# Six places instead of four for split weights, up to the third gate-up block

## The chip, the cores and the metric

One core of a Trainium2 chip runs the kernel. The metric is the device time of one execution in microseconds (us); lower is better. Engines: PE is TensorE (PEld its weight loads), DVE is VectorE, ACT is ScalarE, POOL is GpSimd, SP is SyncE, whose queue issues most of the DMAs.

## The reference

One layer of a decoder trunk with 256 positions and a width of 1024, in float32: three attention branches, a gated merge, and a SwiGLU feed-forward part.

```python
h = rms_norm(x, pre_mix_g[l])
mem_n = rms_norm(mem, mem_norm_g[l])
y = hybrid_mixer(h, mem_n, ...)      # h @ w_in (1024 x 5400), three branches, merge, w_mix_out
x = x + rms_norm(y, post_mix_g[l])
h = rms_norm(x, pre_ffn_g[l])
f = (jax.nn.silu(h @ w_ffn_gate[l]) * (h @ w_ffn_up[l])) @ w_ffn_down[l]   # inner width 2816
x = x + rms_norm(f, post_ffn_g[l])
```

In the mixer the compressed branch of NSA takes its keys and values (the columns `k_c`, `v_c` of `h @ w_in`), joins windows of 32 positions and multiplies them by `cmp_w1` and `cmp_w2`. The selected and window branches, MoBA and the memory branch attend over 256 keys each.

## The kernel before

Every large product has to be more exact than one pass in the fast format (fp32r). So each weight w is split in two fp32r numbers, `wh` (w rounded, written by ACT in `hi`) and `wl` = w - `wh` (written by DVE in `lo`), and the activations likewise (`xh`, `xl`). PE then does three matmuls for one product (`product`, L1120 to L1122): xh by wh, xh by wl, xl by wh.

The weights stream through in units of 1 MB, in one fixed order, on SP's queue, into `raw`, which has `RAW` = 4 slots. A unit is two parts of 256 rows by 512 columns; part v is half of unit v // 2. Part v goes this way: SP loads its unit; ACT makes `wh` in one of `SUBS` = 4 places (`hi`, L474) once the unit has landed (`loaded`) and PE is done with the part that had the place before (`mm_done`); DVE makes `wl` (`lo`, L761); PE multiplies (`sub`, 12 matmuls of 512 columns). A raw slot is free once DVE has split both its parts (`free_slot` on SP).

A block is 512 columns of output. In the first stage each has four parts: block 0 parts 0 to 3, block 1 parts 4 to 7, block 2 parts 8 to 11, and so on. The sums of a block lie in one of two places in PSUM (`acc`), one bank for each tile of 128 positions. ACT copies the bank of tile 0 to `pat` and DVE the bank of tile 1 (`evac_cols`, L556 and L856), and each then raises `ev[0]` or `ev[1]`. PE starts block b only when block b - 2 is copied (`free_acc`).

Each engine runs its own list, written out by hand, in that order alone. `hi_to(v)` and `lo_to(v)` put into ACT's and DVE's list all splits up to part v that are not yet there. In `evac_cols(b)` the first statement is `hi_to(v_last + AHEAD)` (on DVE `lo_to(v_last + AHEAD)`), with v_last the block's last part and `AHEAD` = `SUBS` - 1; the copy stands behind these splits:

```python
v_last = 4 * b + 3
hi_to(v_last + AHEAD)
act.wait_ge(rstd_done, 2 if b >= B_MEMKV else 1)
wait_block(b, 0, v_last)
```

After the first part of block 2 (part 8), PE turns the columns of block 1 that hold `k_c` and `v_c` (`qk_batch(0, 2, ...)`, four 128x128 transposes, L1231). It waits for `ev[0]` and `ev[1]` of block 1 first:

```python
for t in range(TILES):
    pe.wait_ge(ev[t], blocks_ready)
```

The order of loads on SP's queue in this stage is: units 0 and 1 with parts of `gx`, units 2 and 3, `x` (1 MB), units 4 and 5, `memt` (1 MB), units 6 and 7, `mem` (1 MB), units 8 and 9, and `tb` (1.5 MB). Unit 4 waits for the split of unit 0, unit 5 for that of unit 1, and so on. POOL's queue loads `cmp_w1` (2 MB) once block 0 is done. So part 10 is in unit 5, and part 12 in unit 6.

Later stages: 24 attention jobs (`job_plan`) with a gate part between each pair of steps, the merge of branches, the mix block, 11 gate-up blocks in a hardware loop (`ffn_act`, `ffn_dve`, `ffn_body`), and the down projection. At a job n the lists have `hi_to(V_GATE + n + AHEAD)` and `lo_to(V_GATE + n + look_ahead(n))`. `V_GATE` = 24, `V_GU` = 64.

Of the kernel before, what the change touches and what calls it, by code (L numbers as in the profile page):

```python
# [56 lines left out]
ATT_TAIL = ATT_W - 4 * SLICE  # L57
RAW, SUBS = 4, 4
AHEAD = SUBS - 1

# [56 lines left out]
def build_layer(nc, a, out, g_scratch):  # L117
# [13 lines left out]
    with ExitStack() as ctx:  # L131
# [328 lines left out]
        def _(act):  # L460
# [6 lines left out]

            def hi(v, slot, half, w, first_load):

                act.wait_ge(loaded[slot], first_load)  # L470
                if not (isinstance(v, int) and v < SUBS):
                    act.wait_ge(mm_done, v - SUBS + 1)
                k = (2 * slot + half) % SUBS
                nc.scalar.activation(wh[:, k, :, 0:w], raw[:, slot, 2 * half:2 * half + 2, 0:w], ACT.Copy).then_inc(hi_done, 1)  # L474

            def first_hi(k):

                if k < 2:
# [5 lines left out]
                nc.scalar.activation(wh[:, k // 2, k % 2], raw[:, k // 4, k % 4], ACT.Copy).then_inc(hi_done, 1)  # L484
# [43 lines left out]
            for k in range(PIECES):  # L528
                x_hi(k)
                first_hi(k)  # L530
            split[0] = SUBS

# [160 lines left out]
            roots(2, 1, 2)  # L693
            hi_to(V_GU + 3)
            for j in (2, 3):
# [11 lines left out]
            def ffn_hi(i, j, s):  # L707

                v = V_GU + AHEAD + s + 4 * i
                vj = AHEAD + s + 4 * j  # L710
                hi(v, (vj // 2) % RAW, vj % 2, SLICE, ((V_GU + vj) // 2 // RAW + 1) * 32 + (i - j) * 16)

# [4 lines left out]

            def ffn_act(i, j, first):
                for s in range(4):
                    if not first:  # L720
                        ffn_hi(i, j, s)
                    if s == 2 and not first:
                        ffn_ah(i - 1)
# [15 lines left out]
            split[0] = V_GU + 4 * GU_BLOCKS + AHEAD  # L739
            hi_to(V_DOWN + 2 + AHEAD)  # L740
            ffn_ah(GU_BLOCKS - 1)
            nc.scalar.preload_act_table(ACT.Sqrt)
            for n in range(2):
                v_last = V_DOWN + 11 * n + 10
                hi_to(v_last + AHEAD)
# [8 lines left out]
        def _(dve):  # L754
            split = [0]

            def lo(v, slot, half, w):

                dve.wait_ge(hi_done, v + 1 + SUBS)
                k = (2 * slot + half) % SUBS  # L760
                nc.vector.tensor_tensor(wl[:, k, :, 0:w], raw[:, slot, 2 * half:2 * half + 2, 0:w],  # L761
                                        wh[:, k, :, 0:w].bitcast(F32), ALU.subtract).then_inc(lo_done, 1)

            def first_lo(k):

                dve.wait_ge(hi_done, k + 1)
                nc.vector.tensor_tensor(wl[:, k // 2, k % 2], raw[:, k // 4, k % 4], wh[:, k // 2, k % 2].bitcast(F32),
                                        ALU.subtract).then_inc(lo_done, 1)

            def lo_to(v_end):  # L770
                while split[0] <= min(v_end, 2 * UNITS - 1):
                    v = split[0]
                    lo(v, v // 2 % RAW, v % 2, width(v))
                    split[0] += 1
# [47 lines left out]
            for k in range(PIECES):  # L822
                x_lo(k)
                first_lo(k)
            split[0] = SUBS
            dve.wait_ge(bias_row, 1)
# [221 lines left out]
            for t in range(TILES):  # L1048
                gain(0, 0, t, B_MIX)
            lo_to(V_MIX + 7)  # L1050
# [5 lines left out]
            lo_to(V_GU + 1)  # L1056
            round_lo(3, 0)
            lo_to(V_GU + 2)
            sum_halves(0, 1)
# [3 lines left out]
            add_residual(0, 1, 0, 2, x1_done)  # L1063
            lo_to(V_GU + 3)
            add_residual(0, 1, 1, 2, x1_done)
# [15 lines left out]

            def ffn_dve(i, j, first):
                for s in range(4):
                    if not first:
                        ffn_lo(i, j, s)
                    if s == 2 and not first:
                        ffn_al(i - 1)
# [6 lines left out]

            ffn_dve(0, 0, True)
            with nc.vector.Fori(0, (GU_BLOCKS - 1) // 2) as it:
                for j in range(2):
                    ffn_dve(it * 2 + (1 + j), 1 - j, False)
            split[0] = V_GU + 4 * GU_BLOCKS + AHEAD
            lo_to(V_DOWN + 2 + AHEAD)  # L1100
            ffn_al(GU_BLOCKS - 1)
            dve.wait_ge(gpostd, 32)
            lo_to(V_DOWN + 10 + AHEAD)
            for t in range(TILES):
# [11 lines left out]
        def _(pe):  # L1116
# [7 lines left out]
            def sub(v, slot, parity, h, l, k0, w, first, last):  # L1124

                pe.wait_ge(lo_done, v + 1 + SUBS)
                for t in range(TILES):
# [14 lines left out]
            def whole_block(b, v0, subs, h, l, k0=0, w=SLICE, ready=None, after=None):  # L1142
# [3 lines left out]
                for i in range(subs):  # L1146
                    if ready is not None:
                        ready(i)
                    sub(v0 + i, (v0 + i) % SUBS, b % 2, h, l, k0 + 2 * i, w, i == 0, i == subs - 1)
                    for work in (after or {}).get(i, ()):  # L1150
                        work()

            def first_block(after):

                for k in range(PIECES):
                    slot, s = k // 2, k % 2
                    pe.wait_ge(hi_done, k + 1)
# [15 lines left out]
            def by_tiles(b, v0, subs, h, l, k0, ready=None, after=None, first=True):  # L1173
# [3 lines left out]
                for t in range(TILES):  # L1177
                    for i in range(subs):
                        v = v0 + i
                        if t == 0:  # L1180
                            pe.wait_ge(lo_done, v + 1 + SUBS)
                        if ready is not None and i % 2 == 0:
                            pe.wait_ge(tl_done, ready + 2 * t + i // 2 + 1)
                        for s in range(2):
                            ins = product(acc[:, b % 2, t], h, l, k0 + 2 * i + s, t, v % SUBS, s, SLICE,
                                          first and i == 0 and s == 0, i == subs - 1 and s == 1)
# [177 lines left out]
            for n in range(JOBS + 2):  # L1364
# [41 lines left out]
            for n in range(2):  # L1406
                v, b = V_NSA + 2 * n, B_NSA + n
                free_acc(b)
                sub(v, v % SUBS, b % 2, oh, ol, 4, SLICE, True, False)
# [4 lines left out]
                sub(v + 1, (v + 1) % SUBS, b % 2, oh, ol, 6, SLICE, False, True)  # L1414
            whole_block(B_MIX, V_MIX, 4, xh, xl, ready=lambda i: pe.wait_ge(tl_done, i + 1),
# [6 lines left out]
            def ffn_body(i, j, first):  # L1422
# [82 lines left out]
```

## Time and profile before

| what | value |
|---|---|
| time, median of 3 runs | 420.07 us (419.51 to 420.63) |
| the profiled execution's own time | 419.44 us |
| its span, first to last instruction | 417.6 us |
| PE busy | 408.4 us, 98% of the span |
| PEld, DVE, ACT, POOL busy | 328.3, 260.5, 233.5, 40.2 us |
| DMA moved | 78.82 MB, mean 189 GB/s |

The 1.8 us between the span and the profiled time lie ahead of the first and behind the last instruction. A matmul's modelled end overlaps the start of the next, so the step from start to start tells PE's rate: 0.23 us for 512 columns in fp32r.

### The profile page before, as it was taken

What the parts mean: (1) busy time and instruction counts of PE and PEld (TensorE: products, weight loads), DVE (VectorE), ACT (ScalarE), POOL (GpSimd) and SP (SyncE); (2) the same over time, 40 slices, a digit from 0 to 9 for tenths busy, and PEclk for the clock granted to TensorE, in tenths of its full rate; (3) what the DMA queues carried; (4) which work ended last, traced back from release to release, by engine and by line L of the source; (5) the groups of instructions that cost most, each with busy time, mean ns of one, the idle gap of its engine ahead of it and who ended that gap; (6) DMA issues with size and microseconds to landing.
All of it is one profiled execution on the core that took longest, in us unless ns stands there. A gap on an engine that the chain in (4) does not pass through costs nothing.

```text
span 417.6 us, 5875 instructions
## 1 busy us (share of the span) xinstructions
PE 408.4 (98%) x2070; PEld 328.3 (79%) x2070; DVE 260.5 (62%) x450; ACT 233.5 (56%) x402; POOL 40.2 (10%) x76
## 2 busy tenths in 40 slices
PE   8999999999999999999999999999999999999994
PEld 4787889877777777877787788888888888888883
DVE  4854965875776786649859665556555655545434
ACT  5654964577767766744646774544554454545321
POOL 3210020021212122126000000000000000000000
PEclk9999999999999999999999999999999999999999
DMA  8999993535344335366555467556655556666002
GB/s 294 393 335 369 375 334 111 194 112 191 112 152 141 100 104 199 102 239 215 193 173 165 138 227 227 169 176 196 201 178 169 174 185 198 202 202 193 9 0 100
DMA packets 52016, 78.82 MB, mean 189 GB/s; under 512 B 2076, under 2 KB 28488, under 8 KB 51992
## 3 DMA queue, kind: packets, MB, share of 16 engines
q1 hardware_dynamic: 50216, 73.52, 53.7%
q0 software_dynamic: 1344, 4.43, 3.2%
q10 hardware_dynamic: 432, 0.56, 0.4%
q8 instruction: 14, 0.23, 0.2%
q14 instruction: 10, 0.08, 0.1%
HBM read 77.43 MB, written 1.07 MB: 188 GB/s over the span
## 4 chain that ended last, share of the span: by engine, by line
PE 92%; DVE 2%; ACT 2%; DMA 1%; issue 1%; ACTq 0%; DVEq 0%
PE acc L1120 27%; PE acc L1122 26%; PE acc L1121 26%; PE ob L1361 3%; PE sbank L1310 3%; PE ptb L1324 2%; DMA gx<-in_gx 1%; PE ptb L1439 1%; PE acc L1159 1%; PE sbank L1231 1%; PE acc L1163 1%; DVE gates L951 1%; PE acc L1164 1%; DVE xl L796 1%; ACT xh L507 0%
## 5 line engine op out<-in xcount | busy, mean ns | idle before, releaser
L761 DVE TENSOR_TENSOR wl<-raw,wh 128x1024 fp32r<-128x1024 f32 (+1 forms) x126 | 152.7, 1218 | 92.9 <-ACT wh L474 92.4
L474 ACT ACTIVATE wh<-raw 128x1024 fp32r<-128x1024 f32 (+1 forms) x126 | 131.0, 1046 | 92.6 <-PE acc L1122 80.5
L1120 PE MATMUL acc<-wh,xh 128*128 128x512 f32 (+1 forms) x368 | 146.3, 398 | 1.1 <-DVE xl L796 1.1
L1122 PE MATMUL acc<-wh,xl 128*128 128x512 f32 (+1 forms) x368 | 142.2, 386 | 0.0
L1121 PE MATMUL acc<-wl,xh 128*128 128x512 f32 (+1 forms) x368 | 142.0, 386 | 0.0
L1120 PEld LDWEIGHTS acc<-wh,xh 128*128 128x128 f32 x368 | 69.1, 188 | 18.0 <-issue 4.9
L1122 PEld LDWEIGHTS acc<-wh,xl 128*128 128x128 f32 x368 | 69.1, 188 | 14.3
L1121 PEld LDWEIGHTS acc<-wl,xh 128*128 128x128 f32 x368 | 69.2, 188 | 12.5
L1120 PE MATMUL acc<-wh,ah 128*128 128x512 f32 x88 | 34.3, 390 | 0.0
L1122 PE MATMUL acc<-wh,al 128*128 128x512 f32 x88 | 34.3, 389 | 0.0
L1121 PE MATMUL acc<-wl,ah 128*128 128x512 f32 x88 | 34.2, 389 | 0.0
L440 POOL TENSOR_SCALAR sx<-sx,jst 128x256 f32<-128x256 f32 (+1 forms) x48 | 20.2, 433 | 94.2 <-DVE jst L987 52.4
L649 ACT ACTIVATE sx<-sx,jst 128x128 f32<-128x128 f32 (+1 forms) x40 | 17.9, 451 | 5.3 <-DVE jst L979 5.3
L1122 PEld LDWEIGHTS acc<-wh,al 128*128 128x128 f32 x88 | 16.5, 188 | 3.5
L1121 PEld LDWEIGHTS acc<-wl,ah 128*128 128x128 f32 x88 | 16.5, 188 | 3.4
L1120 PEld LDWEIGHTS acc<-wh,ah 128*128 128x128 f32 x88 | 16.5, 188 | 3.3
L731 ACT ACTIVATE silu<-acc,rstd 128x256 f32<-128x256 f32 x22 | 10.3, 475 | 11.8 <-DVE act_tok L1092 8.0
L969 DVE TENSOR_TENSOR sx<-sbank,tb 128x128 f32<-128x128 f32 (+1 forms) x40 | 12.4, 352 | 6.5 <-PE sbank L1310 4.9
L627 ACT ACTIVATE pts<-ptb 128x512 f32<-128x512 f32 x16 | 9.6, 599 | 10.0 <-PE ptb L1324 9.9
L1092 DVE SCALAR_TENSOR_TENSOR act_tok<-acc,rstd,silu 128x256 f32<-128x256 f32 x22 | 10.5, 481 | 6.8 <-ACT silu L731 6.8
L1120 PE MATMUL acc<-wh,oh 128*128 128x512 f32 x32 | 12.9, 402 | 0.0
L677 ACT ACTIVATE tmp<-acc 128x512 f32<-128x512 f32 x8 | 4.8, 600 | 14.2 <-PE acc L1122 14.2
(187 smaller groups left out, 407.0 us busy)
## 6 DMA issues: line engine op xcount, KB each, us to landing
raw<-in_w_in SPq DMA_DIRECT2D x18, 1024.0 KB
raw<-in_w_ffn_gate SPq DMA_DIRECT2D x22, 512.0 KB
raw<-in_w_ffn_up SPq DMA_DIRECT2D x22, 512.0 KB
raw<-in_w_ffn_down SPq DMA_DIRECT2D x22, 512.0 KB
raw<-in_w_mix_out SPq DMA_DIRECT2D x4, 1024.0 KB
raw<-in_w_mem_kv SPq DMA_DIRECT2D x2, 1024.0 KB
raw<-in_w_nsa_o SPq DMA_DIRECT2D x2, 1024.0 KB
raw<-in_w_in SPq DMA_DIRECT2D x3, 512.0 KB, 7.2
```

The source lines that it names most:

```text
L440: ins = nc.gpsimd.tensor_scalar(sx[:, n % 2, lo:hi], sx[:, n % 2, lo:hi], jst[:, 4, n, t:t + 1], 1.0, ALU.mult, ALU.mult)
L474: nc.scalar.activation(wh[:, k, :, 0:w], raw[:, slot, 2 * half:2 * half + 2, 0:w], ACT.Copy).then_inc(hi_done, 1)
L649: ins = nc.scalar.activation(sx[:, n % 2, lo:hic], src[:, n % 2, lo:hic], ACT.Exp, bias=jst[:, 1, n, t:t + 1], scale=SCALE, accum_out=jst[ ...
L731: nc.scalar.activation(silu[:, t], acc[:, j % 2, t, 0:GU_W], ACT.Silu, scale=rstd[:, 3, t:t + 1]).then_inc(silu_done, 1)
L761: nc.vector.tensor_tensor(wl[:, k, :, 0:w], raw[:, slot, 2 * half:2 * half + 2, 0:w], wh[:, k, :, 0:w].bitcast(F32), ALU.subtract).then_in ...
L969: nc.vector.tensor_tensor(sx[:, n % 2, c0:c1], sbank[:, n % 2, c0:c1], tb[:, bh, c1 - c0 - 1::-1], ALU.add).then_inc(dve_c, 1)
L1092: nc.vector.scalar_tensor_tensor(act_tok[:, t], acc[:, j % 2, t, GU_W:2 * GU_W], rstd[:, 3, t:t + 1], silu[:, t], ALU.mult, ALU.mult).then ...
L1120: nc.tensor.matmul(bank[:, 0:w], h[:, k, c], wh[:, slot, s, 0:w], start=first, stop=False)
L1121: nc.tensor.matmul(bank[:, 0:w], h[:, k, c], wl[:, slot, s, 0:w], start=False, stop=False)
L1122: return nc.tensor.matmul(bank[:, 0:w], l[:, k, c], wh[:, slot, s, 0:w], start=False, stop=last)
L1310: ins = nc.tensor.matmul(sbank[:, side, c0:c1], qt[half_rows(side), q, P * t:P * t + P], kt[half_rows(side), k, 0:c1 - c0], start=True, st ...
L1361: ins = nc.tensor.matmul(ob[half_rows(side), c0:c1], v, p, start=(i == 0), stop=(i == count - 1))
```

## The change

The ring of places for split weights has six places (`SUBS` = 6) for all parts up to the end of the third gate-up block, and goes back to four (`FFN_SUBS` = 4) behind it. `AHEAD` goes from 3 to 5, so that ACT and DVE split two parts further ahead in all calls that name `AHEAD`. Calls with a plain number (`hi_to(11)`, `lo_to(15)` and others in the first stage) stay as they are; those at the mix block are written out two parts later. `hi` is given its place and the place's last user. Where `SUBS` stood for the four parts that are split in eight pieces at the start, `IN_PIECES` = 4 stands now. The second and third gate-up blocks are taken out of ACT's and DVE's loops, with 4 and 2 splits (`FFN_PARTS`). `tmp`, which takes what the squares write and nobody reads, shares its place in SBUF with `silu` and `act_tok`. `raw` still has 4 slots, and SP's and POOL's lists are as before.

```diff
-RAW, SUBS = 4, 4
-AHEAD = SUBS - 1
+RAW, SUBS, FFN_SUBS, IN_PIECES = 4, 6, 4, 4
+AHEAD, FFN_AHEAD = SUBS - 1, FFN_SUBS - 1
+FFN_PARTS = [[V_GU + 9, V_GU + 10, V_GU + 11, V_GU + 12], [V_GU + 13, V_GU + 14]]
+def ring(v):
+    w = v - V_GU
+    return w % SUBS if w < 2 * SUBS else w % FFN_SUBS
+def last_user(v):
+    return v - SUBS if v - V_GU < 2 * SUBS + FFN_SUBS else v - FFN_SUBS
-            tmp = sb("tmp", [P, TILES, SLICE], F32, late)
+            with ExitStack() as early:
+                tmp = sb("tmp", [P, TILES, SLICE], F32, early)
-            def hi(v, slot, half, w, first_load):
+            def hi(v, k, slot, half, w, first_load, user):
                 act.wait_ge(loaded[slot], first_load)
-                if not (isinstance(v, int) and v < SUBS):
-                    act.wait_ge(mm_done, v - SUBS + 1)
-                k = (2 * slot + half) % SUBS
+                if not (isinstance(user, int) and user < 0):
+                    act.wait_ge(mm_done, user + 1)
...
-                    hi(v, u % RAW, v % 2, width(v), 32 * (u // RAW + 1))
+                    hi(v, ring(v), u % RAW, v % 2, width(v), 32 * (u // RAW + 1), last_user(v))
...
-            hi_to(V_MIX + 7)
+            hi_to(V_GU + 1)
             squares(0, 1, 0, B_MIX + 1, V_MIX + 7)
...
-            hi_to(V_GU + 1)
+            hi_to(V_GU + 3)
             round_hi(3, 0)
-            hi_to(V_GU + 2)
+            hi_to(V_GU + 4)
...
-            ffn_act(0, 0, True)
-            with nc.scalar.Fori(0, (GU_BLOCKS - 1) // 2) as it:
+            ffn_act(0, 0, True, ())
+            ffn_act(1, 1, False, FFN_PARTS[0])
+            ffn_act(2, 0, False, FFN_PARTS[1])
+            with nc.scalar.Fori(0, (GU_BLOCKS - 3) // 2) as it:
                 for j in range(2):
-                    ffn_act(it * 2 + (1 + j), 1 - j, False)
+                    ffn_act(it * 2 + (3 + j), 1 - j, False)
```

ACT's list around the copies of blocks 0 and 1, before. The first `pat` row is the copy of block 0, the second that of block 1, which stands behind the splits of parts 7 to 10; `gcmp` is what is made of the transposed `k_c` columns:

```order
L525 ACTIVATE small<-ssq,eps 128x2 [waits ssq_done]
L556 ACTIVATE pat<-acc,rstd 128x2x4x64 [waits acc0_done,rstd_done]
L474 ACTIVATE wh<-raw 128x1024 [waits mm_done,loaded3]
L474 ACTIVATE wh<-raw 128x1024 [waits mm_done,loaded0] x2
L474 ACTIVATE wh<-raw 128x1024 [waits mm_done,loaded1]
L556 ACTIVATE pat<-acc,rstd 128x512 [waits acc0_done,rstd_done]
L474 ACTIVATE wh<-raw 128x1024 [waits mm_done,loaded1]
L569 ACTIVATE gcmp<-sbank 64x16x15 [waits qk_pe]
L569 ACTIVATE gcmp<-sbank 64x16x15 x3
L474 ACTIVATE wh<-raw 128x1024 [waits mm_done,loaded2]
L561 ACTIVATE qt<-sbank 128x512 [waits qk_pe]
```

So four splits stand between the two copies, and none between `small` and the copy of block 0. The same stretch of ACT's list in the changed kernel:

```order
L538 ACTIVATE small<-ssq,eps 128x2 [waits ssq_done]
L487 ACTIVATE wh<-raw 128x1024 [waits mm_done,loaded3]
L487 ACTIVATE wh<-raw 128x1024 [waits mm_done,loaded0]
L569 ACTIVATE pat<-acc,rstd 128x2x4x64 [waits acc0_done,rstd_done]
L487 ACTIVATE wh<-raw 128x1024 [waits mm_done,loaded0]
L487 ACTIVATE wh<-raw 128x1024 [waits mm_done,loaded1] x2
L487 ACTIVATE wh<-raw 128x1024 [waits mm_done,loaded2]
L569 ACTIVATE pat<-acc,rstd 128x512 [waits acc0_done,rstd_done]
L582 ACTIVATE gcmp<-sbank 64x16x15 [waits qk_pe]
L582 ACTIVATE gcmp<-sbank 64x16x15 x3
L574 ACTIVATE qt<-sbank 128x512 [waits qk_pe]
```

The splits of parts 11 and 12 moved ahead of the copy of block 1; the one of part 12 waits for `loaded2`, which is unit 6.

DVE's list at the end of the first stage, before, from the copies that end the compressed keys (`ckeys`, `pat<-ob`) to the first step of the compressed softmax (`xc`):

```order
L916 COPY ckeys<-ob 64x15 x2
L919 COPY pat<-ob 32x2x64 x4
L761 TENSOR_TENSOR wl<-raw,wh 128x1024 x2
L856 TENSOR_SCALAR pat<-acc,rstd 128x280
L930 TENSOR_TENSOR xc<-ob,tbc 128x2x4x15
```

The same place in the changed kernel:

```order
L932 COPY ckeys<-ob 64x15 x2
L935 COPY pat<-ob 32x2x64 x4
L777 TENSOR_TENSOR wl<-raw,wh 128x1024 x4
L872 TENSOR_SCALAR pat<-acc,rstd 128x280
L946 TENSOR_TENSOR xc<-ob,tbc 128x2x4x15
```

Four splits instead of two now stand between the copies and the 280 columns of block 5.

## Rows read from the trace of the kernel before

**Rows 1.** The page: busy us of each engine, share of the span, instructions.
```profile
PE 408.4 (98%) x2070; PEld 328.3 (79%) x2070; DVE 260.5 (62%) x450; ACT 233.5 (56%) x402; POOL 40.2 (10%) x76
```

**Rows 2.** Waits of PE, whole span: us in total, times, longest.
```profile
PE acc L1120 <- DVE xl L796: 1.1, 2, 0.7
PE ptb L1280 <- DVE eps L817: 0.9, 1, 0.9
PE sbank L1205 <- DVE yb L955: 0.7, 1, 0.7
PE sbank L1231 <- issue: 0.6, 1, 0.6
PE ptb L1205 <- DVE yb L955: 0.2, 1, 0.2
```

**Rows 3.** Timeline of PE: start, duration, instruction, and idle time before it.
```profile
31.68 0.39 PE L1122 MATMUL acc<-wh,xl 128*128 128x512 f32 x1
32.64 0.41 PE L1231 MATMUL sbank<-const,pat 128*128 128x128 f32 x2 [0.58 <-issue]
```

**Rows 4.** Timeline of ACT, 29 to 41 us.
```profile
29.56 1.06 ACT L474 ACTIVATE wh<-raw 128x1024 fp32r<-128x1024 f32 x1 [4.37 <-DMA raw<-in_w_in]
30.53 0.67 ACT L556 ACTIVATE pat<-acc,rstd 128x512 f32<-128x512 f32 x1
...
33.31 1.55 ACT L569 ACTIVATE gcmp<-sbank 64x240 f32<-64x240 f32 x4 [1.16 <-PE ptb L1231]
39.81 1.06 ACT L474 ACTIVATE wh<-raw 128x1024 fp32r<-128x1024 f32 x1 [4.94 <-DMA raw<-in_w_in]
```

**Rows 5.** Timeline of DVE, 30 to 41 us.
```profile
30.66 1.22 DVE L761 TENSOR_TENSOR wl<-raw,wh 128x1024 fp32r<-128x1024 f32 x1 [3.82 <-ACT wh L474]
31.80 0.74 DVE L856 TENSOR_SCALAR pat<-acc,rstd 128x512 f32<-128x512 f32 x1
...
40.90 1.22 DVE L761 TENSOR_TENSOR wl<-raw,wh 128x1024 fp32r<-128x1024 f32 x1 [5.65 <-ACT wh L474]
```

**Rows 6.** Two stretches: length, busy PE, PEld, DVE, ACT, POOL (count), PEclk, DMA share, GB/s.
```profile
30.00:42.00 12.00, 11.42 (x57) 9.20 (x56) 5.65 (x8) 5.83 (x10) 0.53 (x1) 1.00 1.05 362
240.00:410.00 170.00, 170.00 (x772) 140.67 (x772) 91.02 (x99) 82.43 (x103) 0.00 (x0) 1.00 0.53 167
```

**Rows 7.** DMA issues: queue, count, KB, us to landing; then SP's queue, timeline.
```profile
memt<-in_memt SPq DMA_DIRECT2D x1, 1024.0 KB, 20.6
...
16.49 0.39 SPq L355 DMA_DIRECT2D memt<-in_memt  x1
18.38 11.36 SPq L322 DMA_DIRECT2D raw<-in_w_in  x2
```

**Rows 8.** PE at the start; one chain piece; PE's last matmul; two stretches as rows 6.
```profile
0.94 4.63 PE L1280 MATMUL ptb<-eps 128*128 128x512 f32 x6 [0.94 <-DVE eps L817]
6.34 0.40 PE L1163 MATMUL acc<-wl,xh 128*128 128x512 f32 x1
...
36.04 0.44 PE sbank L1231 x4
...
411.74 0.39 PE L1122 MATMUL acc<-wh,al 128*128 128x512 f32 x1
...
412.20:415.80 3.60, 0.00 (x0) 0.00 (x0) 2.24 (x5) 0.95 (x3) 0.00 (x0) 1.00 0.26 98
415.80:417.60 1.80, 0.00 (x0) 0.00 (x0) 0.00 (x0) 0.00 (x0) 0.00 (x0) 0.51 0.53 199
```

**Rows 9.** Timelines of DVE and PE where the first attention job starts.
```profile
76.45 0.51 DVE L856 TENSOR_SCALAR pat<-acc,rstd 128x280 f32<-128x280 f32 x1
81.24 0.17 DVE L990 RECIPROCAL jst<-jst 128x2 f32<-128x2 f32 x1 [1.05 <-ACT sx L649]
...
80.97 0.60 PE L1231 MATMUL ob<-const,pat 128*128 128x128 f32 x4
84.16 0.49 PE L1324 MATMUL ptb<-const,sx 128*128 128x128 f32 x3
```

More of the change, by code:

```diff
@@ L483, in first_hi @@
                     act.wait_ge(loaded[k // 4], 32)
-                nc.scalar.activation(wh[:, k // 2, k % 2], raw[:, k // 4, k % 4], ACT.Copy).then_inc(hi_done, 1)
+                nc.scalar.activation(wh[:, ring(k // 2), k % 2], raw[:, k // 4, k % 4], ACT.Copy).then_inc(hi_done, 1)
             def hi_to(v_end):
@@ L530, in _ @@
                 first_hi(k)
-            split[0] = SUBS
+            split[0] = IN_PIECES
             def squares_of(i, src, t):
@@ L693, in _ @@
             roots(2, 1, 2)
-            hi_to(V_GU + 3)
+            hi_to(V_GU + 5)
             for j in (2, 3):
@@ L707, in ffn_hi @@
             def ffn_hi(i, j, s):
-                v = V_GU + AHEAD + s + 4 * i
-                vj = AHEAD + s + 4 * j
-                hi(v, (vj // 2) % RAW, vj % 2, SLICE, ((V_GU + vj) // 2 // RAW + 1) * 32 + (i - j) * 16)
+                v = V_GU + FFN_AHEAD + s + 4 * i
+                vj = FFN_AHEAD + s + 4 * j
+                hi(v, vj % FFN_SUBS, (vj // 2) % RAW, vj % 2, SLICE, ((V_GU + vj) // 2 // RAW + 1) * 32 + (i - j) * 16, v - FFN_SUBS)
             def ffn_ah(i):
@@ L716, in ffn_ah, with ffn_act @@
                 nc.scalar.activation(ah[:, bass.ds(i * 2, 2), :], ptb[:], ACT.Copy).then_inc(ah_done, 1)
-            def ffn_act(i, j, first):
+            def ffn_act(i, j, first, parts=None):
                 for s in range(4):
-                    if not first:
+                    if parts is None:
                         ffn_hi(i, j, s)
+                    elif s < len(parts):
+                        hi_to(parts[s])
                     if s == 2 and not first:
@@ L734, in _ @@
             act.wait_ge(rstd_done, 5)
-            ffn_act(0, 0, True)
-            with nc.scalar.Fori(0, (GU_BLOCKS - 1) // 2) as it:
+            ffn_act(0, 0, True, ())
+            ffn_act(1, 1, False, FFN_PARTS[0])
+            ffn_act(2, 0, False, FFN_PARTS[1])
+            with nc.scalar.Fori(0, (GU_BLOCKS - 3) // 2) as it:
                 for j in range(2):
-                    ffn_act(it * 2 + (1 + j), 1 - j, False)
-            split[0] = V_GU + 4 * GU_BLOCKS + AHEAD
-            hi_to(V_DOWN + 2 + AHEAD)
+                    ffn_act(it * 2 + (3 + j), 1 - j, False)
+            split[0] = V_GU + 4 * GU_BLOCKS + FFN_AHEAD
+            hi_to(V_DOWN + 2 + FFN_AHEAD)
             ffn_ah(GU_BLOCKS - 1)
@@ L744, in _ @@
                 v_last = V_DOWN + 11 * n + 10
-                hi_to(v_last + AHEAD)
+                hi_to(v_last + FFN_AHEAD)
                 for t in range(TILES):
@@ L755, in _, with lo @@
             split = [0]
-            def lo(v, slot, half, w):
-                dve.wait_ge(hi_done, v + 1 + SUBS)
-                k = (2 * slot + half) % SUBS
+            def lo(v, k, slot, half, w):
+                dve.wait_ge(hi_done, v + 1 + IN_PIECES)
                 nc.vector.tensor_tensor(wl[:, k, :, 0:w], raw[:, slot, 2 * half:2 * half + 2, 0:w],
@@ L766, in first_lo @@
                 dve.wait_ge(hi_done, k + 1)
-                nc.vector.tensor_tensor(wl[:, k // 2, k % 2], raw[:, k // 4, k % 4], wh[:, k // 2, k % 2].bitcast(F32),
+                nc.vector.tensor_tensor(wl[:, ring(k // 2), k % 2], raw[:, k // 4, k % 4], wh[:, ring(k // 2), k % 2].bitcast(F32),
                                         ALU.subtract).then_inc(lo_done, 1)
@@ L772, in lo_to @@
                     v = split[0]
-                    lo(v, v // 2 % RAW, v % 2, width(v))
+                    lo(v, ring(v), v // 2 % RAW, v % 2, width(v))
                     split[0] += 1
@@ L824, in _ @@
                 first_lo(k)
-            split[0] = SUBS
+            split[0] = IN_PIECES
             dve.wait_ge(bias_row, 1)
@@ L1049, in _ @@
                 gain(0, 0, t, B_MIX)
-            lo_to(V_MIX + 7)
+            lo_to(V_GU + 1)
             sum_halves(0, 0)
@@ L1055, in _ @@
                 add_residual(0, 0, n, 2, x1_done)
-            lo_to(V_GU + 1)
+            lo_to(V_GU + 3)
             round_lo(3, 0)
-            lo_to(V_GU + 2)
+            lo_to(V_GU + 4)
             sum_halves(0, 1)
@@ L1063, in _ @@
             add_residual(0, 1, 0, 2, x1_done)
-            lo_to(V_GU + 3)
+            lo_to(V_GU + 5)
             add_residual(0, 1, 1, 2, x1_done)
@@ L1073, in ffn_lo @@
             def ffn_lo(i, j, s):
-                vj = AHEAD + s + 4 * j
-                lo(V_GU + AHEAD + s + 4 * i, (vj // 2) % RAW, vj % 2, SLICE)
+                vj = FFN_AHEAD + s + 4 * j
+                lo(V_GU + FFN_AHEAD + s + 4 * i, vj % FFN_SUBS, (vj // 2) % RAW, vj % 2, SLICE)
             def ffn_al(i):
@@ L1080, in ffn_al, with ffn_dve @@
                                         ah[:, bass.ds(i * 2, 2), :].bitcast(F32), ALU.subtract).then_inc(al_done, 1)
-            def ffn_dve(i, j, first):
+            def ffn_dve(i, j, first, parts=None):
                 for s in range(4):
-                    if not first:
+                    if parts is None:
                         ffn_lo(i, j, s)
+                    elif s < len(parts):
+                        lo_to(parts[s])
                     if s == 2 and not first:
@@ L1093, in ffn_dve @@
                                                    silu[:, t], ALU.mult, ALU.mult).then_inc(prod_done, 1)
-            ffn_dve(0, 0, True)
-            with nc.vector.Fori(0, (GU_BLOCKS - 1) // 2) as it:
+            ffn_dve(0, 0, True, ())
+            ffn_dve(1, 1, False, FFN_PARTS[0])
+            ffn_dve(2, 0, False, FFN_PARTS[1])
+            with nc.vector.Fori(0, (GU_BLOCKS - 3) // 2) as it:
                 for j in range(2):
-                    ffn_dve(it * 2 + (1 + j), 1 - j, False)
-            split[0] = V_GU + 4 * GU_BLOCKS + AHEAD
-            lo_to(V_DOWN + 2 + AHEAD)
+                    ffn_dve(it * 2 + (3 + j), 1 - j, False)
+            split[0] = V_GU + 4 * GU_BLOCKS + FFN_AHEAD
+            lo_to(V_DOWN + 2 + FFN_AHEAD)
             ffn_al(GU_BLOCKS - 1)
             dve.wait_ge(gpostd, 32)
-            lo_to(V_DOWN + 10 + AHEAD)
+            lo_to(V_DOWN + 10 + FFN_AHEAD)
             for t in range(TILES):
@@ L1124, in sub @@
             def sub(v, slot, parity, h, l, k0, w, first, last):
-                pe.wait_ge(lo_done, v + 1 + SUBS)
+                pe.wait_ge(lo_done, v + 1 + IN_PIECES)
                 for t in range(TILES):
@@ L1148, in whole_block @@
                         ready(i)
-                    sub(v0 + i, (v0 + i) % SUBS, b % 2, h, l, k0 + 2 * i, w, i == 0, i == subs - 1)
+                    sub(v0 + i, ring(v0 + i), b % 2, h, l, k0 + 2 * i, w, i == 0, i == subs - 1)
                     for work in (after or {}).get(i, ()):
@@ L1155, in first_block @@
                 for k in range(PIECES):
-                    slot, s = k // 2, k % 2
+                    slot, s = ring(k // 2), k % 2
                     pe.wait_ge(hi_done, k + 1)
@@ L1180, in by_tiles @@
                         if t == 0:
-                            pe.wait_ge(lo_done, v + 1 + SUBS)
+                            pe.wait_ge(lo_done, v + 1 + IN_PIECES)
                         if ready is not None and i % 2 == 0:
@@ L1184, in by_tiles @@
                         for s in range(2):
-                            ins = product(acc[:, b % 2, t], h, l, k0 + 2 * i + s, t, v % SUBS, s, SLICE,
+                            ins = product(acc[:, b % 2, t], h, l, k0 + 2 * i + s, t, ring(v), s, SLICE,
                                           first and i == 0 and s == 0, i == subs - 1 and s == 1)
@@ L1382, in _ @@
                         free_acc(b)
-                    sub(V_GATE + n, n % SUBS, b % 2, xh, xl, 2 * i, SLICE, i == 0, i == 3)
+                    sub(V_GATE + n, ring(V_GATE + n), b % 2, xh, xl, 2 * i, SLICE, i == 0, i == 3)
                 if n == 0:
@@ L1408, in _ @@
                 free_acc(b)
-                sub(v, v % SUBS, b % 2, oh, ol, 4, SLICE, True, False)
+                sub(v, ring(v), b % 2, oh, ol, 4, SLICE, True, False)
                 if n == 0:
@@ L1413, in _ @@
                     merged_banks(0, 2)
-                sub(v + 1, (v + 1) % SUBS, b % 2, oh, ol, 6, SLICE, False, True)
+                sub(v + 1, ring(v + 1), b % 2, oh, ol, 6, SLICE, False, True)
             whole_block(B_MIX, V_MIX, 4, xh, xl, ready=lambda i: pe.wait_ge(tl_done, i + 1),
@@ L1427, in ffn_body @@
                 for s in range(4):
-                    sub(i * 4 + (V_GU + s), s, j, xh, xl, 2 * s, SLICE, s == 0, s == 3)
+                    slot = ring(4 * i + V_GU + s) if isinstance(i, int) else s
+                    sub(i * 4 + (V_GU + s), slot, j, xh, xl, 2 * s, SLICE, s == 0, s == 3)
                     if s == 1:
@@ L1452, in _ @@
                     v = V_DOWN + 11 * n + i
-                    sub(v, v % SUBS, (B_DOWN + n) % 2, ah, al, 2 * i, SLICE, i == 0, i == 10)
+                    sub(v, ring(v), (B_DOWN + n) % 2, ah, al, 2 * i, SLICE, i == 0, i == 10)
                     if n == 0 and i == 1:
```

## The prediction

> **What bounds the kernel now.** I read the engines' busy times first, then PE's waits, then the timelines of PE, ACT and DVE where PE waits. PE is busy for 408.4 of 417.6 us [rows 1]; the other engines have a third or more of their time free, so what PE does sets the end, and any time in which PE stands adds to it one for one. PE's list of waits is short: five rows, 3.5 us in all [rows 2]. One of them, 0.9 us, is the wait for the very first operand. The other four, 2.6 us, are the most that work done further ahead could give back, and none of the five names a split weight (`wl` or `wh`) as what came last. In the feed-forward stretch from 240 to 410 us PE is busy for 170.00 of 170.00 us [rows 6]. So PE never stands for want of the split weights in what these views show, and a deeper ring for them has nothing there to win.
>
> The row that matters is PE's stop before L1231. Its last matmul of part 8 starts at 31.68 us, the transposes of `k_c` and `v_c` start at 32.64 us, and 0.58 us of it is idle [rows 3]. The profile calls it "issue", but the code says what PE waits for: the copies of block 1 on ACT and on DVE. ACT waits 4.37 us for unit 5 to land, splits part 10 from 29.56 us, and copies from 30.53 us [rows 4]; DVE splits part 10 from 30.66 us and copies from 31.80 to 32.54 us [rows 5]. PE goes on 0.10 us later. The reader sees here a copy that is late only because it stands in an in-order list behind a split whose data have not landed. From the start of ACT's last split ahead of the copy to PE's restart it is 32.64 - 29.56 = 3.08 us.
>
> **The change, part by part.** *ACT and DVE around block 1.* The change puts the splits of parts 11 and 12 ahead of the copy of block 1, as the order of ACT's list shows. Part 11 is in unit 5, as part 10 is, and costs one split. Part 12 is in unit 6. ACT splits it before at 39.81 us, after 4.94 us of idle time that ends with the landing [rows 4], so 39.81 us is when unit 6 landed. Does the change bring unit 6 earlier? The list on SP's queue is the same. The unit needs slot 2, free after the split of part 5, which stands where it stood; SP issued it at 18.38 us, behind `memt`, issued at 16.49 us with 20.6 us to land, so at 37.1 us [rows 7]. The DMA engines are full over this stretch, with a busy share of 1.05 from 30 to 42 us [rows 6]. Unit 6 comes 2.7 us behind `memt` on a queue that is full, and nothing that the change moves is ahead of it. I take 39.81 us, and 0.7 us to either side.
>
> The tail of the chain is the same as before: the last split on ACT, then the last split on DVE, then DVE's copy, then PE. So PE restarts at 39.81 + 3.08 = 42.89 us instead of 32.64 us. **Term 1: +10.25 us.** Since L1231 stands in PE's list ahead of parts 9 to 11, all of PE's work is behind it, and nothing of PE's can be done meanwhile. The 0.58 us of before is inside the 10.25, not beside it.
>
> *PE's clock after the stop.* PE would stand from about 32.07 (31.68 + 0.39) to 42.89 us, 10.8 us. No such stop is in the trace before, but its end and its start bound the cost. After the last matmul, which ends at about 412.13 us, the granted clock stays at 1.00 up to 415.80 us and is then 0.51 [rows 8], 3.7 us behind PE's last work. A stop of 10.8 us is nearly three times that, so I expect the lower level, 1.2 GHz, at the restart. How long does it last? At the start, six matmuls of 512 columns on `eps` begin in 0.94 us and take 4.63 us, 0.77 us or more each; four transposes of the same plain float32 kind with 128 columns take 0.44 us in the chain at 36.04 us, 0.11 us each, which is 0.44 us for 512 columns [rows 8]. The first six thus run at half speed, and full speed is there at 6.34 us at the latest, after at most 5.4 us of work. Work done at half speed for 5.4 us costs 2.7 us more than at full speed; for the 4.63 us, 2.3 us. The bounds are 0 (the level does not fall) and 2.7 us; since rows 8 show both the fall and the slow start, I take the upper half, 2.4 us. **Term 2: +2.4 us.**
>
> By the Trainium skill (TensorE: Matmul & The Clock Gate, HAM oscillation), a long wait for DMA between matmuls drops the array to half clock, and the matmuls after it run cold. The trace shows the drop only at its end, where nothing follows; no row before shows a cold restart in mid-kernel. Without that rule and without rows 8 the sum would be 2.4 us less.
>
> *Blocks 0 and 2 to 4.* Block 0 now waits for part 8, in unit 4. PE needs that copy only at block 2, some 5 us later: 0. The copy of block 2 waits for part 16 in unit 8; DMA goes on during PE's stop and so is 10 us further against PE: 0. In ACT's and DVE's lists between there are calls with plain numbers, which keep their reach, so the copy of block 3 comes in a bunch of four splits. Each is about 1.2 us on DVE [rows 5]; two more than before, 2.4 us, of which the delay of PE's restart hides most. I take 0, with 1 us as the upper bound.
>
> *Block 5 and the first job.* DVE now has two more splits ahead of the copy of block 5, 2 x 1.2 = 2.4 us. That copy starts at 76.45 us, the reciprocal of job 0 comes at 81.24 us, and PE turns job 0 at 84.16 us; the transposes of `q_x` at 80.97 us want the copy of block 5 and the end of `xc` [rows 9]. In DVE's own list the reciprocal moves by some 1.8 to 2.4 us, to 83.4 at the latest, and GpSimd's scaling and a hand-over after it take about 1 us: 84.4 against 84.16. So this is nearly all in the slack. **Term 3: +0.1 us**, bounds 0 and 1.5.
>
> *The rest.* From job 1 on each call does as many splits as before, since the lead was gained once; each still waits for the same `mm_done`, because the reach and the number of places grow by the same 2. The waits for `yb` and `xl` (0.7, 0.2 and 1.1 us) [rows 2] come from copies and sums that the change does not touch: 0, and at most 2.0 us to gain. `raw` has four slots and each slot is freed two parts earlier and needed two parts earlier: 0. `tmp` has no reader, so a shared place costs 0. The unrolled gate-up blocks have 6 splits instead of 8 in a stretch where PE never stands: 0; if that cover were gone, a split on ACT is 1.06 us [rows 4].
>
> **Sum.** 10.25 + 2.4 + 0.1 = 12.75 us on the profiled execution's 419.44 us: 432.2 us. The median of the runs is 0.63 us above that execution (420.07 against 419.44), so the median after is 432.8 us, 3.0% slower.
>
> **The rivals.**
> A. *As above*, a stop of about 10 us and a slow restart: 432.8 us. Chance 0.70.
> B. *The stop without the slow restart*: the clock's fall needs more than 10.8 us, or full speed is back at once. 420.07 + 10.35 = 430.4 us. For it: nothing shows a fall in mid-kernel. Against it: the 3.7 us at the end. Chance 0.10.
> C. *The late bunches cost too*: the copy of block 3 or of block 5 is late for PE, by up to 1 and 1.5 us: up to 435.3 us. For it: DVE's slack at job 0 is used up. Against it: PE is later by all of the first stop. Chance 0.10.
> D. *Unit 6 lands sooner*, since a place for a split and so a slot comes free earlier somewhere, and the stop is 3 to 8 us: 423 to 430 us. Against it: part 5, and all that is ahead of unit 6, stand where they stood. Chance 0.05.
> E. *Faster*: the deeper lead gives back waits for split weights that hide in the modelled ends, and the copy of block 1 is not late. Its place is L1231; it needs unit 6 before about 29 us, so that 3.08 us later PE is not held at 32.1 us. Then the most is the 2.6 us of rows 2: 417.5 us. Chance 0.03. *No change* is the same with nothing to give back: 420.1 us, 0.02.
>
> A difference under 0.3% (1.3 us) is about what a measurement of this kernel cannot tell from none. Slower has 0.95 (A to D), the same 0.02, faster 0.03. The likeliest case by itself spans 431.2 to 434.0 (unit 6 by 0.7 us, the clock by 1.1 and 0.3). The range takes in B and most of C: 429.8 to 435.0 us.
>
> **What the profile after would show.** Term 1: ACT's copy of block 1 behind a split that ends an idle stretch "<-DMA raw<-in_w_in" at about 39.8 us, DVE's copy at 42.0 us, PE idle for some 10.8 us before the transposes of `pat` at 42.9 us. Term 2: a granted clock well under 1.00 from about 36 us, and matmuls of 512 columns 0.43 us apart for up to 5 us behind the restart. Term 3: no stop of PE over 0.3 us between 60 and 110 us of before's time. The rest: waits for `yb` and `xl` as in rows 2, and a last stretch of 170 us as full as before. It would be wrong if unit 6 landed at another time, or if another engine's list had room that I took for order.

## The result and the profile after

| | before | changed |
|---|---|---|
| median | 420.12 us (419.51 to 420.63, 4 runs) | 431.85 us (431.59 to 432.25, 4 runs) |
| profiled execution, span | 419.44, 417.6 us | 431.59, 429.8 us |
| mean granted clock | 0.998 | 0.984 |

The changed kernel takes 1.029 times as long (95% interval 1.0278 to 1.0303). Four executions among the experiments below took 600 to 2190 us and are left out of every number: the other runs of the same kernels agree within 2 us.

PE's waits in the changed kernel (us in total, times, longest), beside [rows 2]:

```profile
PE sbank L1251 <- issue: 10.6, 1, 10.6
PE acc L1140 <- DVE xl L812: 1.2, 2, 0.7
PE ptb L1300 <- DVE eps L833: 0.9, 1, 0.9
PE sbank L1225 <- DVE yb L971: 0.7, 1, 0.7
PE ptb L1225 <- DVE yb L971: 0.2, 1, 0.2
```

Four of the five rows are those of before to 0.1 us. The one before the transposes of `pat` went from 0.6 to 10.6 us. What ends the wait is called "issue", so the row doesn't tell the cause; the timelines of ACT, DVE and PE do (start, duration, instruction, idle time before it):

```profile
29.23 2.01 ACT L487 ACTIVATE wh<-raw 128x1024 fp32r<-128x1024 f32 x2 [3.92 <-DMA raw<-in_w_in]
39.49 1.06 ACT L487 ACTIVATE wh<-raw 128x1024 fp32r<-128x1024 f32 x1 [8.25 <-DMA raw<-in_w_in]
40.46 0.67 ACT L569 ACTIVATE pat<-acc,rstd 128x512 f32<-128x512 f32 x1
...
40.58 1.22 DVE L777 TENSOR_TENSOR wl<-raw,wh 128x1024 fp32r<-128x1024 f32 x1 [7.90 <-ACT wh L487]
41.73 0.74 DVE L872 TENSOR_SCALAR pat<-acc,rstd 128x512 f32<-128x512 f32 x1
...
31.60 0.39 PE L1142 MATMUL acc<-wh,xl 128*128 128x512 f32 x1
42.57 0.66 PE L1251 MATMUL sbank<-const,pat 128*128 128x128 f32 x2 [10.58 <-issue]
```

ACT splits parts 10 and 11 from 29.23 us and then waits 8.25 us for unit 6. The copy of block 1 (L569) stands behind it, though its sums were ready long before (in experiment 6 ACT copies them at 28.02 us). In [rows 4] the same copy was at 30.53 us. From the start of the last split to PE's restart it is 42.57 - 39.49 = 3.08 us, to the hundredth as before.

The clock, in stretches of the changed kernel (columns as in [rows 6]; PEclk, the granted clock, is the third number from the end):

```profile
37.10:37.20 0.10, 0.00 (x0) 0.00 (x0) 0.00 (x0) 0.00 (x0) 0.00 (x0) 0.99 1.00 369
37.20:37.30 0.10, 0.00 (x0) 0.00 (x0) 0.00 (x0) 0.00 (x0) 0.00 (x0) 0.50 1.08 389
46.00:47.00 1.00, 1.00 (x4) 0.79 (x3) 0.00 (x0) 0.00 (x0) 0.00 (x0) 0.50 1.05 387
48.00:49.00 1.00, 1.00 (x8) 0.85 (x7) 0.00 (x0) 0.30 (x1) 0.00 (x0) 1.00 1.07 369
250.00:420.00 170.00, 170.00 (x772) 140.74 (x771) 88.82 (x95) 81.30 (x102) 0.00 (x0) 1.00 0.51 161
```

It falls at 37.2 us, while PE stands (its last matmul ended at 31.99 us), and PE restarts at 1.2 GHz (0.50). Matmuls of 512 columns begin 0.43 us apart, and 0.23 us apart once the clock is back at 2.4 GHz:

```profile
46.02 0.63 PE L1140 MATMUL acc<-wh,xh 128*128 128x512 f32 x1
46.45 0.63 PE L1141 MATMUL acc<-wl,xh 128*128 128x512 f32 x1
...
47.60 0.39 PE L1141 MATMUL acc<-wl,xh 128*128 128x512 f32 x1
47.83 0.39 PE L1142 MATMUL acc<-wh,xl 128*128 128x512 f32 x1
48.06 0.60 PE L1251 MATMUL sbank<-const,pat 128*128 128x128 f32 x4
```

From the restart to the next transposes it is 48.06 - 42.57 = 5.49 us. Before, the transposes that follow the row at 32.64 us in [rows 3] stand here in PE's timeline:

```profile
35.88 0.60 PE L1231 MATMUL sbank<-const,pat 128*128 128x128 f32 x4
```

That was 35.88 - 32.64 = 3.24 us. So the two terms are 42.57 - 32.64 = 9.93 us and 5.49 - 3.24 = 2.25 us. Together they are 12.18 us, and the profiled executions are 12.15 us apart, so nothing else is left to explain. The places further on say the same:

```profile
93.15 0.60 PE L1251 MATMUL ob<-const,pat 128*128 128x128 f32 x4
94.97 0.17 DVE L1006 RECIPROCAL jst<-jst 128x2 f32<-128x2 f32 x1 [1.05 <-ACT sx L662]
96.34 0.49 PE L1344 MATMUL ptb<-const,sx 128*128 128x128 f32 x3
```

Beside [rows 9] both PE rows are 12.18 us later. DVE's reciprocal is 13.73 us later, so DVE is indeed 1.55 us behind at job 0, inside its slack.

### The profile page after: what moved, and what is told of

Its sections match the earlier page's. It is cut to its first block, busy times and chain, and to the rows that moved or that the text cites. A ratio compares the mean times of both kernels' runs of the same rounds, so it can differ in the third digit from the quotient of the medians.

```text
span 429.8 us, 5846 instructions
## 1 busy us (share of the span) xinstructions
PE 410.5 (96%) x2070; PEld 330.1 (77%) x2070; DVE 260.4 (61%) x450; ACT 233.1 (54%) x402; POOL 40.1 (9%) x76
## 4 chain that ended last, share of the span: by engine, by line
PE 85%; DMA 8%; DVE 2%; issue 2%; ACT 2%; SPq 1%; DVEq 0%; ACTq 0%
PE acc L1140 25%; PE acc L1142 24%; PE acc L1141 24%; DMA raw<-in_w_in 5%; DMA x<-in_x 3%; PE ob L1381 3%; PE sbank L1330 2%; PE ptb L1344 2%; PE ptb L1460 1%; PE sbank L1251 1%; DVE gates L967 1%; DVE xl L812 1%; ACT xh L520 0%; ACT wh L487 0%; PE ob L1267 0%
## 5 line engine op out<-in xcount | busy, mean ns | idle before, releaser
L1251 PE MATMUL sbank<-const,pat 128*128 128x128 f32 x22 | 3.7, 288 | 10.6 <-issue 10.6
```

## Experiments

Theory: the list order is the whole loss. A split that waits for a late unit stands ahead of a copy, PE waits for the copy, and the stop lowers the clock. Rivals: the ring of six itself costs or gains, or the slow clock costs nothing.

**1. Part 12 behind the copy of block 1, six places.**

```diff
-                hi_to(v_last + AHEAD)
+                hi_to(11 if b == 1 else v_last + AHEAD)
-                lo_to(v_last + AHEAD)
+                lo_to(11 if b == 1 else v_last + AHEAD)
```

> The changed kernel, but ACT's and DVE's lists have only the splits up to part 11 ahead of the copy of block 1; part 12 (unit 6) comes behind it. Theory (the copy is late because a split that waits for unit 6 stands ahead of it): PE's stop of 10.6 us before the transposes goes to about 1.5 us (part 11 adds one split of DVE, 1.2 us, less the end of a matmul), the clock stays at 1.00, and the time is about 421.0 us, 0.9 us above the kernel before. Rival (the deeper ring costs elsewhere: later bunches of splits, the unrolled blocks, more SBUF traffic): the stop goes but the time stays above 423 us. Rival (the deeper ring gives something that the stop hid): under 419.5 us.

423.34 us (422.91 to 424.17). The big stop is gone, 8.5 us of the time with it, but 4.0 us are left against the median of the kernel before that was timed beside it (419.38 us), where 0.9 was forecast. The trace of this run, PE at the start, then ACT and PE around the stop, and a stretch behind the restart:

```profile
9.70 0.73 PE L1179 MATMUL acc<-wh,xh 128*128 128x512 f32 x2 [0.97 <-ACT wh L497]
...
30.83 2.01 ACT L487 ACTIVATE wh<-raw 128x1024 fp32r<-128x1024 f32 x2 [4.39 <-DMA raw<-in_w_in]
...
35.05 0.42 PE L1251 MATMUL sbank<-const,pat 128*128 128x128 f32 x2 [2.14 <-issue]
39.87 0.60 PE L1251 MATMUL sbank<-const,pat 128*128 128x128 f32 x4
...
35.30:38.70 3.40, 3.40 (x12) 2.73 (x11) 1.62 (x4) 1.49 (x4) 0.52 (x1) 0.50 1.06 387
```

The forecast had a stop of about 1.5 us and the clock at 1.00. Unit 5 landed 1.3 us later than before (30.83 against 29.56 us in [rows 4]) and part 11 adds its split, so the stop was 2.14 us, and the clock was at half for 3.4 us behind it (PE took 39.87 - 35.05 = 4.82 us to the next transposes, against 3.24 us). PE also waited at the start, at 9.70 us, which the profile before does not show. The time alone fits the rival as well, which said over 423 us, so this run didn't clear the ring.

Three of the nine executions of the kernel before that were timed beside this run took 422.2 us, at a granted clock of 0.992 to 0.996. No trace was taken of them. A stop like this one, behind a late unit 5, would fit, but that is not shown.

**2. The kernel before, four places, part 12 ahead of the copy.** The same two lines with 12 in the place of 11.

> The kernel before, with four places and all else as it was, but with the splits up to part 12 ahead of the copy of block 1 in both lists. Theory (the order of the two lists alone makes the loss): PE restarts at 42.6 us, and the time is 432.0 us, as that of the changed kernel within 0.5 us. Rival (the six places or the reach in other blocks carry a part of it): under 430 us.

432.21 us (431.36 to 432.35), within 0.4 us of the changed kernel's time. ACT and PE in this run:

```profile
39.89 1.06 ACT L474 ACTIVATE wh<-raw 128x1024 fp32r<-128x1024 f32 x1 [7.34 <-DMA raw<-in_w_in]
...
42.97 0.45 PE L1231 MATMUL sbank<-const,pat 128*128 128x128 f32 x1 [11.15 <-issue]
```

Again 3.08 us from one to the other. Moving the splits of parts 11 and 12 in two lists, with no ring of six anywhere, makes the whole loss; and it is part 12 that ACT waits 7.34 us for.

**3. PE kept busy in the stop.** The result of the added matmuls is read by nobody.

```diff
             def qk_batch(beta, blocks_ready, sources):
+                if beta == 0:
+                    for _ in range(10):
+                        nc.tensor.matmul(ptb[:, 0:512], still[:, 0:P], still[:, 0:512], start=True, stop=True)
```

> The changed kernel, and PE does 10 more matmuls of 512 columns in plain float32 on eps (8.5 us at full speed) between part 8 and the transposes that wait; their result is read by nobody. Theory (after the stop PE works at half speed for 4.9 us, which costs 2.25 us): the transposes still start at 42.6 us, the granted clock stays at 1.00, and the time falls by 2.2 us to 429.6 us. Rival (the slow stretch costs nothing, since PE waits for ACT and DVE in it anyway): 431.8 us.

Three runs gave 429.48, 429.55 and 431.35 us, the last at a granted clock of 0.993 against 0.996 and 0.998. Ten matmuls left 2.24 us of the stop idle. With 12 matmuls:

> As the run with 10 matmuls in the stop, with 12 (10.2 us), so that next to nothing of the stop is idle. Theory (half speed after the stop costs 2.25 us): granted clock 1.00 throughout, transposes at 42.6 us, 429.6 us, 2.2 us under the changed kernel. Rival (the slow stretch costs under 1 us): 431 us or more.

429.60 us (five runs from 429.44 to 429.72). PE's timeline and the stretch behind it:

```profile
31.87 10.51 PE L1240 MATMUL ptb<-eps 128*128 128x512 f32 x24
42.68 0.41 PE L1254 MATMUL sbank<-const,pat 128*128 128x128 f32 x2 [0.30 <-issue]
45.91 0.60 PE L1254 MATMUL sbank<-const,pat 128*128 128x128 f32 x4
...
43.00:50.00 7.00, 7.00 (x37) 5.81 (x36) 2.85 (x5) 3.31 (x7) 0.53 (x1) 1.00 1.06 379
```

PE restarts 0.11 us later than in the changed kernel, at full clock, and takes 45.91 - 42.68 = 3.23 us to the next transposes instead of 5.49 us. That is 2.26 - 0.11 = 2.15 us less, and the profiled executions are 431.59 - 429.44 = 2.15 us apart. By the medians it is 2.25 us, or 1.9 us if each is set against the kernel before as it was timed beside it. The second term of the sum is shown by itself.

**4. Unit 6 ahead of `memt` on SP's queue, six places.**

```diff
+            plain(6, w_in, 0, SLICE * 3)
             sp.dma_start(memt0[:], memt).then_inc(memtd, 16)
-            projection(3)
+            plain(7, w_in, 4, SLICE * 3)
```

> The changed kernel, but SP's queue has unit 6 ahead of memt instead of behind it. Theory (PE restarts 3.1 us after unit 6 lands): unit 6 lands at about 36.8 us instead of 39.5 us, PE restarts at 39.9 us, and the time is lower by 2.7 us, at 429.2 us; the clock still falls for about 5 us. Rival (unit 6 isn't what the copy waits for, but the split of part 11 or a part of the queue of PE): 431.8 us.

428.49 us (427.95 to 428.97). ACT's split of part 12 and PE's restart:

```profile
36.76 1.06 ACT L488 ACTIVATE wh<-raw 128x1024 fp32r<-128x1024 f32 x1 [5.91 <-DMA raw<-in_w_in]
...
39.84 0.66 PE L1252 MATMUL sbank<-const,pat 128*128 128x128 f32 x2 [7.59 <-issue]
```

Unit 6 lands 2.73 us sooner, and PE restarts 2.73 us sooner, 3.08 us behind it. The profiled executions are 431.59 - 428.97 = 2.62 us apart, so the time falls with the landing. The medians are 3.36 us apart, where 2.7 was forecast. The three runs that were not profiled had a granted clock of 0.991 against 0.984 in the profiled one, so their slow stretch may have been shorter; no trace shows it.

**5. The copy of block 1 behind part 9, four places.** The two lines of experiment 1 with 9.

> The kernel before with four places, but the copy of block 1 stands behind the splits up to part 9 instead of 10, so that it no longer waits for unit 5. Theory (PE's 0.58 us of idle time and 0.74 us from start to start before the transposes are the same effect as the loss, on a small scale): the wait goes and the time falls by 0.7 us to 419.4 us. Rival (another wait takes its place at the next operand, since part 10 is split later): no change, 420.1 us.

419.27 us against 419.58 us, a ratio of 0.9989 (0.998 to 0.9998). PE's wait before the transposes is gone from its list. The profiled execution still took 419.42 us, since another wait was in its start:

```profile
9.66 0.73 PE L1159 MATMUL acc<-wh,xh 128*128 128x512 f32 x2 [0.95 <-ACT wh L484]
```

By the interval of the ratio the gain is between 0.1 and 0.8 us, at the edge of what can be measured. The forecast time of 419.4 us was met, but in part by luck: it was worked out as 0.7 us under 420.1 us, and the kernel before took 419.58 us beside this run, 0.3 us more.

**6. The same with six places.**

> The changed kernel with six places, but the copy of block 1 stands behind the splits up to part 9. Theory (the two further parts of lead are worth nothing beside the loss at block 1): the same as the kernel before with the same order, 419.4 us within 0.3 us. Rival (the lead gives back hidden waits): 418.5 us or less. Rival (the bunch of four splits ahead of the copies of blocks 3 and 5 costs): 420 us or more.

423.89 us (422.9 to 424.21): a miss. ACT, PE and the stretch behind:

```profile
47.49 1.06 ACT L487 ACTIVATE wh<-raw 128x1024 fp32r<-128x1024 f32 x1 [2.96 <-DMA raw<-in_w_mem_kv]
48.45 0.67 ACT L569 ACTIVATE pat<-acc,rstd 128x512 f32<-128x512 f32 x1
...
50.69 0.63 PE L1251 MATMUL sbank<-const,pat 128*128 128x128 f32 x4 [3.02 <-issue]
...
51.30:54.70 3.40, 3.40 (x10) 2.65 (x9) 2.72 (x8) 3.35 (x7) 0.06 (x1) 0.50 1.09 361
```

The same thing one block later: the copy of block 2 stands behind part 16, which is in unit 8 (`w_mem_kv`), and unit 8 lands at 47.49 us. In the changed kernel the first stop had given DMA 10 us to get ahead, and hid this one: there ACT's three splits ahead of that copy end no wait for a DMA.

```profile
52.39 2.94 ACT L487 ACTIVATE wh<-raw 128x1024 fp32r<-128x1024 f32 x3
55.24 0.68 ACT L569 ACTIVATE pat<-acc,rstd 128x512 f32<-128x512 f32 x1
```

**7. Block 1 behind part 9, block 2 behind part 15, six places.**

> The changed kernel, with the copy of block 1 behind the splits up to part 9 and the copy of block 2 behind those up to part 15, so that neither waits for a unit that lands later (unit 8 landed at 47.5 us in the last run, and its split stood ahead of the copy of block 2). Theory (the 4.3 us that were left with block 1 alone are the same mechanism at block 2: 3.2 us of stop and 1.7 us of half clock): PE has no stop over 0.3 us before 190 us, the clock stays at 1.00, and the time is 419.4 us. Rival (a bunch of splits ahead of the copies of blocks 3 and 5 holds PE too): 420 to 422 us, with a stop near 57 or 82 us.

423.29 us (421.79 to 423.38), a second miss. ACT and PE:

```profile
56.46 0.67 ACT L487 ACTIVATE wh<-raw 128x560 fp32r<-128x560 f32 x1 [2.73 <-DMA raw<-in_w_in]
57.03 0.67 ACT L569 ACTIVATE pat<-acc,rstd 128x512 f32<-128x512 f32 x1
...
58.66 0.76 PE L1251 MATMUL sbank<-const,pat 128*128 128x128 f32 x4 [2.10 <-ACT pat L569]
...
59.10:62.40 3.30, 3.30 (x10) 2.62 (x9) 0.77 (x3) 2.88 (x5) 0.00 (x0) 0.50 0.72 267
```

Now it is the copy of block 3, behind part 20 in unit 10. The stop is where the rival put it, near 57 us, but it is no bunch of splits: ACT is idle for 2.73 us until unit 10 lands. The copies of blocks 1, 2 and 3 each had the trap, each hidden by the one before it.

**8. Six places, and the first stage's copies behind the same parts as in experiment 5.**

```diff
-                hi_to(v_last + AHEAD)
+                hi_to({0: 6, 1: 9, 2: 14, 3: 18}.get(b, v_last + AHEAD))
```

The same on DVE with `lo_to`.

> Six places, but in the first stage the splits ahead of the copies of blocks 0 to 3 reach only as far as with four places (parts 6, 9, 14, 18); from block 4 on the lead is 5. Theory (the two further parts of lead give nothing by themselves, since PE never waits for a split weight): 419.3 us, as the kernel before with the copy of block 1 first (419.27). Rival (the longer lead saves hidden waits in the later stages): 418.5 us or less. Rival (it costs there): over 420 us.

419.36 us (11 runs from 419.16 to 419.46), ratio 0.9988 (0.9979 to 0.9997). With four places, in experiment 5, it was 0.9989. The ring of six and its longer lead from block 4 on neither cost nor give anything that can be measured.

**9 and 10. Other splits that stand ahead of a copy.** DVE's merges of the two NSA output blocks get one split less ahead of them, first with four places (and block 1 behind part 9), then with six (and experiment 8).

```diff
             def merge(b):
-                lo_to(v_last + AHEAD)
+                lo_to(v_last + AHEAD - (b >= B_NSA))
```

> The kernel before with four places; the copy of block 1 stands behind part 9, and at the two NSA output blocks DVE merges behind one split less. Theory (an in-order list with a split ahead of a copy holds PE there too: 0.83 and 0.41 us from start to start before the transposes of yb): both stops of PE for yb go, and the time is 419.27 - 1.2 = 418.0 us. Rival (the split that was put behind is then late for PE, or the next wait, for xl, grows by as much): 419.2 us.

> The run with six places and the old reach in the first stage, and the same move of one split behind the two merges. Theory (the lead isn't needed for that): 418.0 us, as with four places. Rival (only the longer lead can afford a split put behind): with six places at least 0.5 us faster than with four.

Four places: 417.97 us (417.8 to 418.01), ratio 0.9958 (0.9942 to 0.9973). Six: 418.13 us (five runs from 417.93 to 418.25), ratio 0.9961 (0.9946 to 0.9977). None of these five was profiled, so only the times of experiment 10 are read. PE's waits with four places:

```profile
PE acc L1120 <- DVE xl L796: 1.2, 2, 0.7
PE ptb L1280 <- DVE eps L817: 0.9, 1, 0.9
PE acc L1120 <- DVE wl L761: 0.6, 1, 0.6
```

Both rows for `yb` are gone. A new row shows up: the split weights of part 12, at 42.0 us. The gain did not need the deeper ring.

**11. Experiment 9 and unit 6 ahead of `memt`.**

> The four-place kernel with the copy of block 1 and the merges first (417.97 us), and unit 6 ahead of memt on SP's queue. There PE still stops once in the first stage, at part 12: 0.95 us from start to start, 0.6 us of it idle, for the split weights of unit 6, which lands at 39.8 us. Theory (in the first stage the landing of units is what is late): the stop goes, and the time is 417.3 us. Rival (memt or unit 7, now later, is waited for instead): 418 us or more.

417.05 us (416.79 to 417.27), ratio 0.9929 (0.9905 to 0.9954) against the kernel before. PE's waits:

```profile
PE acc L1121 <- DVE xl L797: 1.1, 2, 0.7
PE ptb L1281 <- DVE eps L818: 0.9, 1, 0.9
PE acc L1160 <- ACT wh L485: 0.2, 1, 0.2
```

The wait for `wl` is gone. The row for `wh` is a wait of 0.2 us at 5.4 us, in the start; the rival's stop for `memt` or unit 7 did not come. This is the fastest of all, with four places, and beats both kernels.

## Why the prediction was right

The median was forecast at 432.8 us with a range of 429.8 to 435.0; it is 431.85 us. The likeliest case's own range was given as 431.2 to 434.0; the terms named for it (0.7 us for unit 6, 1.1 and 0.3 us for the clock) add up to 431.0 to 433.8. The result lies in both.

- **Term 1**, forecast 10.25 us: 9.93 us. The mechanism, the place and the 3.08 us of the chain held; unit 6 landed at 39.49 us instead of 39.81 us. Experiments 2 and 4 show it from both sides.
- **Term 2**, forecast 2.4 us: 2.25 us in the trace, and 1.9 to 2.26 us by the run with 12 matmuls in experiment 3. Rival B is out. The half clock at the restart was argued from [rows 8] and came true. The size was picked as the upper half of 0 to 2.7 us and not worked out, so that it came this close is in part luck. The clock fell at 37.2 us, 5.2 us behind PE's last matmul, where about 36 us was forecast.
- **Term 3**, forecast 0.1 us: nothing. DVE was 1.55 us behind at job 0, where 1.8 to 2.4 us was forecast, and PE never waited for it. Rival C is out.
- **Blocks 2 and 3**, forecast 0: right for the changed kernel. For block 2 the reason given held, that DMA gets ahead in the first stop. For block 3 the text looked only at a bunch of splits, and missed that its copy waits for unit 10. It did not say either that without the stop at block 1 the others would cost about 4 us (experiments 6 and 7). Rival E thus needed more than its condition at L1231: units 8 and 10 would probably have been next, though no run has unit 6 that early.
- **The deeper ring gives nothing**: shown by experiment 8 against 5, and by 10 against 9.
- **At most 2.6 us to gain**, from the idle times in [rows 2]: too low. Experiments 5, 9 and 11 removed the rows for `pat` and `yb`, 1.5 us of idle time, and the gain of experiment 11 is 2.7 us (1.9 to 4.0) with the 1.1 us for `xl` still there. A row of waits counts the idle time alone: at L1231 that is 0.58 us, while the step from start to start in [rows 3] is 0.96 us against the usual 0.23.
- **The sum** was 0.6 us over the profiled execution (432.2 against 431.59). The shift from that execution to the median, 0.63 us, was a term that didn't carry over: in the changed kernel it is 0.26 us. The two, 0.6 and 0.37 us, make up the 0.95 us but for rounding.

## What to carry to other kernels

In an in-order list, "further ahead" puts work that waits for a distant thing ahead of work that somebody needs now. Before lengthening a lead, list for each copy which load the last split ahead of it waits for, and when that load lands in the trace of before. Such stops hide one another, so a repair has to cover every place of the stage and not only the one that the profile shows. The deeper ring was worth nothing here, and PE's waits in [rows 2] have no row for a split weight; the list order and the order of loads were worth 0.7%.

## What the runs showed of the hardware

Stops of PE of 2.14 us (experiment 1), 3.02 us (experiment 6) and 2.10 us (experiment 7) were each followed by 3.3 to 3.4 us at half clock, which began only after PE had gone on (35.05, 50.69 and 58.66 us against stretches from 35.30, 51.30 and 59.10 us). The one stop that the rows before show with a fall behind it is 3.7 us long [rows 8], and experiment 1's forecast had the clock stay at 1.00. A stop of 2.24 us in the profiled run of experiment 3 was followed by none:

```profile
42.73 0.41 PE L1254 MATMUL sbank<-const,pat 128*128 128x128 f32 x2 [2.24 <-issue]
...
42.00:44.00 2.00, 1.26 (x8) 1.17 (x9) 1.22 (x3) 0.59 (x2) 0.53 (x1) 1.00 1.03 395
44.00:47.00 3.00, 3.00 (x17) 2.49 (x16) 1.03 (x3) 1.33 (x4) 0.00 (x0) 1.00 1.05 387
```

So the length of the stop alone doesn't decide it; what does is open. The cost is out of proportion: in experiment 1 PE took 4.82 us from restart to the next transposes instead of 3.24, 1.6 us on top of a stop of 2.1 us.
